# A two-layer mixer block: low weight parts and S5 tables on VectorE, Silu at the projection, the delta rule's norms beside its convolution

## The reference

```
def second_block(x, ...):
    h = rmsnorm(x, norm1_w); p = h @ w_in
    (a_u, a_v, b_b, b_c, b_h, c_q, c_k, c_v, c_a, c_b, c_z,
     d_q, d_k, d_v, d_g, d_z) = jnp.split(p, split_idx, axis=-1)
    ...
def deltanet_mixer(q, k, v, a, b, z, conv_w, a_log, dt_bias, norm_w):
    qkv = silu(causal_dwconv(concatenate([q, k, v]), conv_w))      # 4 taps
    q, k, v = split(qkv, 3); q, k = l2norm(to_heads(q)), l2norm(to_heads(k))
    g = -exp(a_log) * softplus(a + dt_bias); beta = sigmoid(b)
    o = chunk_gated_delta_rule(q, k, v, g, beta)     # chunks of 64, a state between them
    return rmsnorm(o, norm_w) * silu(z)
def gla_mixer(q, k, v, g_lr, z, ...):                # gated linear attention, chunks of 64
    ...
    return rmsnorm(o, norm_w) * silu(z)
def s5_branch(u, ...):                               # complex diagonal recurrence
    abar = exp(dt * a); bb = f(abar, a) * b          # tables: powers of abar times b and c
    y = scan(...) ; y = gelu(y); return y * sigmoid(y @ glu_w + glu_b)
```

## Time and the profile before

| | us |
|---|---|
| runs | 2642.49, 2644.53, 2646.07 |
| median | 2644.53 |
| the profiled execution | 2651.53 |
| its span | 2649.7 |
| PE busy | 2486.3 (94%) |
| DVE busy | 1191.1 (45%) |
| ACT busy | 568.3 (21%) |
| POOL busy | 610.9 (23%) |

### The profile page before, as it was taken

The page is one execution under the profiler, slowest core; times in us unless marked ns, Lnnn a source line. Parts: engine busy times, 40 slices in busy tenths (PEclk is TensorE's granted clock), DMA queues, the critical chain, the costliest instruction groups (busy, mean ns, idle before and its releaser), DMA issues.

```text
span 2649.7 us, 36492 instructions
## 1 busy us (share of the span) xinstructions
PE 2486.3 (94%) x15202; PEld 2067.3 (78%) x15202; DVE 1191.1 (45%) x1968; ACT 568.3 (21%) x889; POOL 610.9 (23%) x303
## 2 busy tenths in 40 slices
PE   5699999999999999999999897778999999999998
PEld 5588788888777788888787885667778888888887
DVE  7692138784697623232522535562432222222224
ACT  4111111214321112232233334431210000000002
POOL 2495123230000222201200100012323333333330
PEclk9799999999999999999999998898999999999999
DMA  7436434236466733431332522112311111111101
GB/s 254 127 132 188 161 116 136 83 112 199 135 208 210 235 111 135 143 112 32 129 127 96 172 78 94 34 38 96 104 32 48 47 47 48 47 47 47 47 24 63
DMA packets 226900, 284.70 MB, mean 107 GB/s; under 512 B 31857, under 2 KB 144466, under 8 KB 226770
## 3 DMA queue, kind: packets, MB, share of 16 engines
q1 hardware_dynamic: 194514, 234.48, 27.5%
q10 hardware_dynamic: 32256, 48.35, 4.9%
HBM read 200.89 MB, written 81.89 MB: 107 GB/s over the span
## 4 chain that ended last, share of the span: by engine, by line
PE 77%; DVE 12%; ACT 3%; DMA 3%; issue 3%; SPq 1%; POOL 0%; ACTq 0%; DVEq 0%; POOLq 0%
PE PS L491 22%; PE PS L3046 18%; PE PS L494 16%; PE PS L3063 9%; PE PS L668 1%; PE PS L1835 1%; PE PS L1815 1%; DVE T L954 1%; DMA LAR<-ret_d 1%; DVE W_LO L409 1%; DVE T L955 1%; DVE SGS L2962 1%; PE PS L1156 1%; DVE XN L629 1%; PE PS L2353 1%
## 5 line engine op out<-in xcount | busy, mean ns | idle before, releaser
L441 POOL TENSOR_SCALAR W_HI<-RAW 128x2048 fp32r<-128x2048 f32 (+1 forms) x66 | 130.8, 1988 | 1391.1 <-PE PS L491 544.7
L491 PE MATMUL PS<-W_HI,OP_HI 128*128 128x512 f32 (+1 forms) x1184 | 308.9, 405 | 19.2 <-issue 9.2
L491 PE MATMUL PS<-W_LO,OP_HI 128*128 128x512 f32 (+1 forms) x1184 | 289.9, 387 | 0.0
L491 PE MATMUL PS<-W_HI,OP_LO 128*128 128x512 f32 (+1 forms) x1184 | 286.8, 384 | 0.0
L491 PEld LDWEIGHTS PS<-W_HI,OP_HI 128*128 128x128 f32 x1184 | 221.1, 196 | 66.8 <-issue 13.5
L491 PEld LDWEIGHTS PS<-W_LO,OP_HI 128*128 128x128 f32 x1184 | 222.6, 191 | 45.6
L491 PEld LDWEIGHTS PS<-W_HI,OP_LO 128*128 128x128 f32 x1184 | 219.5, 188 | 43.7
L3119 DVE TENSOR_TENSOR AB<-PS,GSB 128x512 f32<-128x512 f32 x44 | 30.4, 691 | 391.0 <-ACT GSB L3102 391.0
L515 ACT ACTIVATE OST<-PS 128x512 f32<-128x512 f32 (+2 forms) x164 | 94.5, 576 | 520.2 <-PE PS L494 279.8
L494 PE MATMUL PS<-OP_HI,W_HI 128*128 128x512 f32 (+1 forms) x768 | 190.4, 391 | 6.8 <-DVE W_LO L409 6.8
L447 POOL TENSOR_TENSOR W_LO<-RAW,W_HI 128x2048 fp32r<-128x2048 f32 x39 | 184.0, 4717 | 42.9 <-DVE W_LO L409 39.7
(11 more groups left out here) (445 smaller groups left out, 3436.5 us busy)
## 6 DMA issues: line engine op xcount, KB each, us to landing
RAW<-in_w_in SPq DMA_DIRECT2D x28, 1024.0 KB, 5.8
RAW<-in_w_gate_up SPq DMA_DIRECT2D x44, 512.0 KB, 4.7
RAW<-in_w_out SPq DMA_DIRECT2D x12, 1024.0 KB, 8.8
RAWD<-in_w_down SPq DMA_DIRECT2D x11, 1024.0 KB, 4.9
X<-x_d SPq DMA_DIRECT2D x4, 2048.0 KB, 8.9
x_d<-X SPq DMA_DIRECT2D x2, 4096.0 KB, 16.2
ptok_d<-OST ACTq DMA_DIRECT2D x24, 256.0 KB, 2.0
pch_d<-OST ACTq DMA_DIRECT2D x24, 256.0 KB, 2.0
```

What stands on the lines that cost most here:

```text
L441: nc.gpsimd.tensor_scalar(hi, raw, 1.0, 1.0, ALU.mult, ALU.mult).then_inc(*w_hi.by(1))
L491: ins = nc.tensor.matmul(PS[:, bank, 0:width], act_part[:, k, (g.tile0 + a) * P:(g.tile0 + a + 1) * P], w_part[:, slot, k, 0:width], start ...
```

## The change

It has four parts, in one diff.

1. **Prologue and tables.** DVE makes the low parts of all of the first 16 weight halves; POOL only casts `W_HI`. The `CPW` tables move from POOL to DVE (`outputs` in `dve_s5_tables`), behind the second, third and fourth slice of `XPW`. The S5 parameters are loaded by ACT's queue, x's tiles come earlier on SP's, and the parameters' turns on PE and their copies go from ahead of `u` to behind its first unit. The first unit of `xk` waits for its operands pass by pass. The norm's tiles are planned at 6 + 4.8 a tile instead of 15 + 3.6. `U8`, `BCTq`, `UTq` and `URq` have buffers of their own, and the Toeplitz stores stand between the `BCTq` loads.
2. **Convolution.** DVE sums two groups before the first turn and stays ahead; PE turns a half group after every `ptok` unit. ACT squares q and k there (`SQJ`), DVE sums the squares (`dve_delta_norms`), and one root serves all pairs. Silu of both z is taken when the projection is stored. The short convolution is later.
3. **Pairs.** The four squares, sums and roots and `act_z` are gone; `DZ` has two buffers. The decays of the next pair are made one step earlier. `VV` stays in its PSUM bank and the product is added to it, so that L2357 falls away. GLA's three cumulated sums are waited for one by one.
4. **Weights of `out2`.** POOL waits for the last `SGS` before it casts the first half, and DVE makes the low parts of the first four.

```diff
-    DVE_HALVES = (0, 1, 2, 3, 4, 6, 8)
-    BOTH_HALVES = 10
+    DVE_HALVES = tuple(range(16))
+    BOTH_HALVES = 17
...
-    LATER_HALVES = tuple(... ("pch", 1, 2), ("ptok", 0, 3))
+    LATER_HALVES = tuple(... ("pch", 1, 2), ("ptok", 0, 3), ("out2", 0, 2))
...
             if b == gemms["out2"].first_block and half == 0:
                 pool.wait_ge(*gl["kv"](NPAIR))
+                pool.wait_ge(*gl["s"](8 * NPAIR))
...
+            if n == 0 and first_hi:
+                last, have = b, width // P
+                by_pass = ([w_hi(2 * b + 2), first_hi(have)], [w_split(2 * b + 2)], [operand[0](operand[1] + have)])
...
-    XK_START, XK_UNIT, XV_START, XV_UNIT = 18.0, 2.95, 42.0, 5.5
+    XK_START, XK_UNIT, XV_START, XV_UNIT = 18.0, 3.5, 46.0, 6.2
+    NORM_START, NORM_TILE, NORM_LATE = 6.0, 4.8, 3.4
...
+        def outputs(i):
+            if i:
+                dve.wait_ge(*s5_out(32 * i))
+            src = CP[:, :, pairs, :]
+            for n in range(SC):
+                chain(V.tensor_tensor(T12[:, 0], src, spread(0), MUL))
+                chain(V.tensor_tensor(T12[:, 1], src, spread(6), MUL))
+                V.tensor_tensor(CPW[:, 0, :, n, :], T12[:, 0, 0], T12[:, 1, 1], SUB).then_inc(*s5_cpw.by(1))
+                V.tensor_tensor(CPW[:, 1, :, n, :], T12[:, 0, 1], T12[:, 1, 0], ADD).then_inc(*s5_cpw.by(1))
...
+            if i < NSL - 1:
+                dve_low_part(dve, (LOW_FIRST, LOW_FIRST + 1, LOW_FIRST + 2)[i])
+            if i >= 1:
+                outputs(i - 1)
+            if i == NSL - 2:
+                dve_low_part(dve, LOW_FIRST + 3)
...
-    U8 = at("U8", "stage", 8192, [P, SC, P])
-    BCTq = at("BCTq", "stage", 12288, [P, 2, 2, 2, P])
+    U8 = at("U8", "extra", 4096, [P, SC, P])
+    BCTq = at("BCTq", "extra", 8192, [P, 2, 2, 2, P])
...
-        return 1.0 + 1.45 * n
+    CONV_SUM = (0.6, 0.7, 1.8, 3.8, 5.8, 7.8)
+    CONV_SILU = (-0.3, 1.3, 4.3, 6.3, 8.3, 10.2)
+    def turn_time(m):
+        return m + 0.7
...
+                if m < NSQ:
+                    if m >= 2:
+                        act.wait_ge(*dc_ss(m - 1))
+                    act.activation(SQJ2[m % 2][:, :], PS[:, 7, :], ACT.Square).then_inc(*dc_sq.by(1))
...
-        def act_z(self, act, u, z):
-            act.activation(self.ZS[:, :, :], z, ACT.Silu).then_inc(*self.zs.by(1))
...
-                if k < 5:
-                    for r in halves_of:
-                        T.matmul(PS[r, 1, :], ident[r, r], VV[r, :, :].rearrange("p n c -> p (n c)"), start=True, stop=False)
...
-                            ins = T.matmul(PS[r, 1, n * GD:(n + 1) * GD], now[r, n, :], P1[r, n, :], start=False,
-                                           stop=n == 2 * GH - 1)
+                            ins = T.matmul(PS[r, 2, n * GD:(n + 1) * GD], now[r, n, :], P1[r, n, :], start=False,
+                                           stop=n == 2 * GH - 1, skip_group_check=True)
...
-            yield pair_time(u, -0.5) if u == 0 else level_time(u - 1, 5) + 4
+            yield pair_time(u, -0.5) if u == 0 else level_time(u - 1, 5) + 1.5
...
-        return pair_time(0, -0.5 + 38.5 * u + x)
+        return pair_time(u, x)
...
+                silu={0: (C_CZ - C_CA, C_DG - C_CA), 2: (C_DZ - C_DV, C_TOK - C_DV)}), act_conv(act), act_delta_root(act), ...
```

More of the change, by code:

```diff
@@ L412, in dve_split_first @@
     def dve_split_first(dve, times):
-        for r, time in zip(DVE_HALVES, times):
+        for r, time in enumerate(times):
             yield time
             dve_low_part(dve, r)
-    LATER_HALVES = tuple(r for name, n, m in (("glu", 1, 1), ("out_s5", 0, 3), ("xo", 1, 1), ("pch", 1, 2), ("ptok", 0, 3))
+    LATER_HALVES = tuple(r for name, n, m in (("glu", 1, 1), ("out_s5", 0, 3), ("xo", 1, 1), ("pch", 1, 2), ("ptok", 0, 3), ("out2", 0, 2))
                          for r in range(2 * (gemms[name].first_block + n), 2 * (gemms[name].first_block + n + m)))
@@ L574, in act_norm_root, with act_norm_tiles @@
         act.activation(st[:, o + 16 + t:o + 17 + t], st[:, o + 8 + t:o + 9 + t], ACT.Sqrt).then_inc(*st_b.by(1))
-    def act_norm_tiles(act, q, start, ready, turned_too=True, free={}):
+    def act_norm_tiles(act, q, start, ready, turned_too=True, free={}, late=0.0):
         for i in range(TT + 3):
@@ L586, in act_norm_tiles @@
             if turned_too and i >= 3:
-                yield start + i + 1.3
+                yield start + i + 1.3 + (late if i - 3 in free else 0.0)
                 if i - 3 in free:
@@ L606, in dve_scaled_inplace, with dve_norm_tiles @@
                                        ALU.mult, ALU.mult).then_inc(*inplace.by(1))
-    def dve_norm_tiles(dve, q, chain, start):
+    def dve_norm_tiles(dve, q, chain, start, late=0.0):
         for i in range(1, TT + 3):
@@ L623, in dve_norm_tiles @@
             if i >= 3:
-                yield start + i + 1.3
+                yield start + i + 1.3 + (late if i - 3 >= TT - 2 else 0.0)
                 dve_lo(dve, q, i - 3)
@@ L1129, in sp_s5_in, with sp_s5_toeplitz @@
             sp.dma_start(BCTq[:, m % 2], bct_d[:, 2 * m:2 * m + 2, :, :]).then_inc(*s5b_bs[m % 2].by(16))
+    def sp_s5_toeplitz(sp):
+        for i in range(SC):
+            yield s5_in_time(i + 1) + 0.45
+            if i == 0:
+                sp.wait_ge(*s5_rsb(2 + NSL))
+            rows = SP_ * (i + 1)
+            sp.dma_start(toep_d[0:rows, i, :], RSB[P - rows:P, :]).then_inc(*s5_out.by(16))
+        yield s5_in_time(PARTS)
+        sp_columns(sp)
     def pe_s5_in(pe):
@@ L3212, in _ @@
         def _(pool):
[L3213 to L3220 removed]
+            pool_split(pool, 0, len(halves))
             pool_ffn(pool)
@@ L3225, in _ @@
             together(act_first(act), act_s5_params(act),
-                     paced(act_norm_tiles(act, 1, 0, lambda t: nx_in[t // 2](16), free={TT - 2: mm_done(gemms["xv"].end)}), 15, 3.6),
+                     paced(act_norm_tiles(act, 1, 0, lambda t: nx_in[t // 2](16), free={t: mm_done(gemms["xv"].end) for t in (TT - 2, TT - 1)}, late=NORM_LATE), NORM_START, NORM_TILE),
                      paced(act_gemm_store_steps(act, "xk", lambda b, a, h, w: ka_d[(4 * b + a) * P:(4 * b + a + 1) * P, :]),
```

349 lines of the change are left out of this document (164 added, 185 removed).

## The result

The changed kernel takes 2610.5 us (median of 4 runs, 2605.5 to 2612.3) against 2643.5 of before (2642.5 to 2646.1): a ratio of 0.9865 (0.9853 to 0.9878), 33 us less. In a second series it took 2613.0 us, 0.9865 (0.9848 to 0.9883). The forecast was 2582.5 in a range of 2560 to 2612. So the sign was right and the size too large by about 28 us. That the time lies in the range is partly luck: the first series is 1.5 us inside its upper end, the second 1 us outside it.

The account below looks back on a forecast made before the run. PE, holding 77% of the last chain, was taken as the bound, with time to win where it idles or drops work. From 2651.5, -27 - 2 - 8 - 25 = -62 gave 2589.5 profiled, 2582.5 median; range 2560 to 2612.

Parts of the forecast that it names:

- Prologue: Stage up to u's first pass: PE's waits on low parts, C parameters and last operands go; -27, bounds -18 and -36.
- could cost 1 to 3 us at some tiles: Prologue: DVE's nine more halves there and in the tables, and the norm's chain feeding PE with little to spare.
- Tables: S5 table stage: DVE's 64 steps fit inside PE's 144 us and PE's short idle time goes; -2, or up to +20.
- the second rival: Prologue and tables: DVE becomes the bound, +15 to +20 in this stage, so 2600; chance 0.14, with or without the first rival.
- Convolution: Convolution beside the projection: PE's waits of 5.6 and 1.6 and its slower passes go; -8, bounds -3 and -10.
- Pairs: Delta and GLA pairs: waits on roots, low parts, turns and decays go, and work is dropped; -25 with out2's start.
- L2357: Pairs: 18.0 us of PE work dropped, partly turning into waiting between P's product and DVE's answer; -5, bounds 0 and -16.
- `SGS`: Pairs: wait of 8.9 us shrinks as POOL's cast waits for it; -5, only -3 if VT is urgent there.
- `DTE` and `VT`: Change of pairs: waits of 2.8 and 4.5 us shrink as the decays are made one step earlier; -4.
- the first rival: Pairs bound by latency give back what was freed, convolution becomes ACT's; pairs -8, convolution -3, so 2604; chance 0.16.
- Out2: Start of out2: the table load and Silu of z behind its last turn go; -2, summed within the pairs' -25.
- The 7.0 between the profiled execution and the median: Whole kernel: profiled execution of before, 2651.5, against the runs' median, 2644.5; taken off at the end of the sum.

Follow-up runs that it names:

- e1: The kernel before once more, no edit, with a second profile; timed 2644.9 us, ratio 0.9997.
- e4: After, with the weight loads of the gret projection planned later on SP's queue, so four table stores no longer stand behind a waiting load; 2603.1 us, ratio 0.9848.
- e9: The changed kernel once more, no further edit, with a second profile; timed 2613.0 us.
- e5: After, with the identity product of VV (L2357 of before) put back behind each P product; 2603.7 us, ratio 0.9846.
- e10: After with later weight loads on SP's queue and out2's first low parts behind VT and SD, plus the identity product of VV put back; 2589.1 us, ratio 0.9786.
- e12: After with all four mends: later weight loads, out2's low parts behind VT, identity product back, XN first in DVE's prologue order; 2591.2 us, ratio 0.9799.
- e11: After with later weight loads and later out2 low parts, plus DVE's prologue order changed so XN goes first; 2590.5 us, ratio 0.9790.
- e6: After, with DVE's first two low parts of out2 moved behind VT and SD of the last pair; 2598.9 us, ratio 0.9826.
- e8: After with both later weight loads on SP's queue and out2's first low parts behind VT and SD; 2591.1 us, ratio 0.9787.
- e3: Before with parts 2 to 4 of the change alone (convolution, pairs, out2's weights); 2625.7 us, ratio 0.9931.
- e2: Before with part 1 of the change alone (prologue, tables, own buffers, Toeplitz stores); 2626.4 us, ratio 0.9937.
- e7: Before with only the convolution's order changed (sums ahead, a turn per ptok unit, later short convolution); norms and Silus as before; 2639.4 us, ratio 0.9977.

## Why the prediction came out as it did

Most of the waits that were named went away, and the sum was too large: -62 forecast, -39 between profiles, -33 timed. By its own steps, against the means of the two profiles each:

- **Prologue, -27 forecast, -23.0 measured.** The waits behind low parts and C parameters and the 9.2 ahead of `u` went as said, and the first turn came at 10.0 instead of 16.3 (14.7 in e1). The new work that "could cost 1 to 3 us at some tiles" was named and left out of the sum. It is the step that was mis-sized: behind the first turn PE waits 14.7 us for `XN` in after, where it waited 5.6 before (6.9 in e1), 8 to 9 us more.
- **Tables, -2 forecast, +6.6 measured.** This is the step that failed in kind. I priced DVE's steps at 1.44 us, and they took 1.45; and I found 8 us of slack at the fourth slice. But I did not look at the second slice, nor at what waits in SP's queue. The low part that a weight load waits for had moved from POOL, where it ended 34 us behind the start of `u`, to DVE, behind two slices of tables, where it ended 43 us behind it. The first stores of `BTa`, due near 117, went out at 135.5, and ACT and PE needed them. It resembles the second rival (which named stores behind which DVE must wait), but DVE was not the bound and waited for no store: the wait was ACT's and PE's. e4 shows it, and the five kernels with the queue mended show what the term is without it: 153.6 in the mean against 155.7, the -2 of the forecast.
- **Convolution, -8 forecast, -5.8 measured** in the URy to HAT column. Of these, 2.2 lie ahead of the convolution, where nothing was changed, and only 3.6 in its own stretch (144.9 us in the mean of before and e1, 141.3 of after and e9). So part of the agreement is luck. The waits on `CAC` and `OV` went, beside them the clock is full, and ACT kept up with the groups. What the term lacked is the wait on `GTB` behind the later load, 1.7 us in after and 5.1 in e9.
- **Pairs, -23 forecast without out2, -15.0 measured.** The waits on `VV` and `TRA` gave what was said. Three terms were wrong. L2357 was given -5 between 0 and -16; it is worth 0 (e5, e10, e12 against e11). `SGS` was given -5, and -3 "if `VT` is urgent there": it was. The wait of 8.9 went, but a stall of 5.0 us stands in its place, with a low clock behind it, and without it the last pair is some 7 us shorter (e6). `DTE` and `VT` were given -4: the 2.8 of `DTE` went, but the waits on `VT` grew from 4.5 to 13.7. So the first rival described the pairs rightly in part: what was won at one place is waited for on `P` and `VT`.
- **Out2, -2 forecast, -1.7 measured.**
- **The 7.0 between the profiled execution and the median** was subtracted as if it stayed. It was this execution's excess. In a difference it has no place, and the forecast for the median would have been the same 62 below; and the rows that I summed came from an execution at the upper end, whose waits and slow passes are somewhat too dear.
- **Table loads.** The four loads for Silu of z are in the trace of after, with 1.28 us each and the next operation right behind, as I took them. No wait of PE in the stage ends on them. So no drain as the Trainium skill counts it (ScalarE: Activation LUTs, "What ACT_TABLE_LOAD costs") shows here:

```profile
1553.07 1.28 ACT L524 ACT_TABLE_LOAD   x1
1554.36 0.38 ACT L524 ACTIVATE OST<-PS 128x256 f32<-128x256 f32 x1
```

## What to carry to other kernels

When work moves to another engine, list what waits for its result in every queue, and what stands behind those waits. The price of the work itself was right to 1%, and the loss was one load that waited ahead of four stores. The load of `ADT` behind the short convolution is the same thing once more, on a smaller scale. Of work dropped on the busiest engine, only that counts which isn't in the shadow of a hand-over: if the engine waits at the next step anyway, little or nothing is won. A stage is to be read in more than one execution before a few microseconds of it are explained, and cut where the edit begins: 6 us of the convolution's column also stood in a kernel without its edit. And a stage that is bound by hand-overs should not have large pieces of other work put between two links of its chain, even on an engine that is idle half the time: moving one such piece was worth 12 to 14 us (e6). With the queue's order mended as well (e8) it was about 20, more than half of what the change itself brought.

## What the runs showed of the hardware

The granted clock in the pairs is 0.97 to 0.98 in the three kernels with the identity product in this version (e5, e10, e12) and 0.88 to 0.93 in the seven without it (after, e3, e4, e6, e8, e9, e11). The product alone does not keep the clock up: before's pairs have it too, with more waits around it, and are at 0.91 to 0.94 (before, e1, e2, e7). The 64 matmuls are busy 16.6 us in e10, but they raise PE's busy time by only 3.5 us there (against e8) and 6.4 in e12 (against e11), since the other matmuls became shorter. I hadn't expected that dropping work lowers the clock enough to cancel most of what it saves.

A low part on DVE took 3.90 us instead of 2.28 (the one at 1756.20) when it met the second of POOL's two casts. The casts ended at 1746.27; by my estimate a low part that stands until then and takes its 2.28 would end at 1748.55, and this one ended at 1748.41. The Trainium skill (SBUF — State Buffer, "Who interferes with whom") says that such a pair blocks fully, and here the trace agrees. Without POOL beside it, `SGS` took 2.03 us for the same eight operations that took 11.81 across two of POOL's low parts.
